# HGRN value unit moved behind the scores of the fourth NSA pair in the third block's mixer stage

## What is computed

```
h = x @ w_in
(q_n, kc, vc, ks, vs, kw, vw, g_n, q_m, k_m, v_m, conv_in, q_h, f_h, i_h, g_h) = jnp.split(h, split_points, axis=-1)
o_nsa  = nsa_attention(q_n, kc, vc, ks, vs, kw, vw, gates, rel_tab[:NSA_HEADS])
o_conv = conformer_conv(conv_in, dw_w, dw_b, cln_g, cln_b, pw_w)
o_hgrn = hgrn2_mixer(q_h, f_h, i_h, g_h, lb, hn_g)      # i_h: the values
mixed  = jnp.concatenate([o_nsa, o_moba, o_conv, o_hgrn], axis=-1) @ w_out
```

## Time and profile before

| what | value |
|---|---|
| median of 3 runs | 3122.36 us (3117.55 to 3126.65) |
| the profiled execution | 3120.94 us, its span 3119.1 us |
| TensorE matmul busy | 2967.4 us (95%) |
| DVE, ACT, POOL busy | 55%, 46%, 5% |
| mean granted TensorE clock | 0.97 of full |
| instructions | 53947 |

### The profile page before, as it was taken

One profiled execution on the slowest core, in us unless ns is written; L12 is line 12 of the kernel. 1 busy time (PEld: TensorE's weight loads), 2 busy tenths in 40 slices (PEclk: granted clock), 3 DMA queues, 4 the chain that ended last, 5 costly groups with the idle time before them and its releaser, 6 DMA issues.

```text
span 3119.1 us, 53947 instructions
## 1 busy us (share of the span) xinstructions
PE 2967.4 (95%) x23720; PEld 2757.1 (88%) x23720; DVE 1717.3 (55%) x2029; ACT 1434.4 (46%) x1831; POOL 164.1 (5%) x197
## 2 busy tenths in 40 slices
PE   8999998999999998999999999999889999999998
PEld 8988898999989898998989899898879899886887
DVE  5455555455454555455456654546685555474555
ACT  4455654445455654444445444444441344344444
POOL 1000100000000100001000000000010000054000
PEclk9999999999999999999999999999989999898999
DMA  6553334554543344555554455454320255340443
GB/s 244 186 187 127 131 137 162 189 189 176 189 176 136 122 145 165 187 182 215 189 200 166 151 186 188 177 189 150 136 82 4 84 180 187 142 164 32 156 178 135
DMA packets 69394, 492.89 MB, mean 158 GB/s; under 512 B 7853, under 2 KB 9421, under 8 KB 10534
## 3 DMA queue, kind: packets, MB, share of 16 engines
q1 hardware_dynamic: 64224, 465.53, 41.5%
q10 hardware_dynamic: 4938, 23.92, 2.0%
HBM read 488.32 MB, written 1.06 MB: 157 GB/s over the span
## 4 chain that ended last, share of the span: by engine, by line
PE 82%; DVE 8%; ACT 6%; POOL 2%; issue 2%; PEld 1%; DMA 0%; PEldq 0%; ACTq 0%; DVEq 0%; POOLq 0%; SPq 0%
PE bank L105 52%; PE acc L105 29%; ACT weights_hi L118 2%; DVE weights_lo L313 2%; POOL conv_gate L3102 1%; POOL conv_out L3105 1%; DVE tmp L673 1%; DVE h L666 1%; DVE h L681 1%; PEld acc L105 0%; DVE b_x_lo L733 0%; DVE b_x_lo L505 0%; PE acc L1005 0%; DMA weight_ring<-in_weights 0%; DVE tmp L613 0%
## 5 line engine op out<-in xcount | busy, mean ns | idle before, releaser
L313 DVE TENSOR_TENSOR weights_lo<-weight_ring,weights_hi 128x2048 fp32r<-128x2048 f32 x440 | 1009.7, 2295 | 946.1 <-ACT weights_hi L118 945.7
L105 PE MATMUL bank<-b_x_hi,weights_hi 128*128 128x256 f32 x3576 | 1017.7, 285 | 22.0 <-DVE b_x_lo L733 17.2
L105 PE MATMUL bank<-b_x_hi,weights_lo 128*128 128x256 f32 x3576 | 1012.3, 283 | 0.0
L105 PE MATMUL bank<-b_x_lo,weights_hi 128*128 128x256 f32 x3576 | 1011.6, 283 | 0.0
L118 ACT ACTIVATE weights_hi<-weight_ring 128x2048 fp32r<-128x2048 f32 x440 | 839.5, 1908 | 371.0 <-PE acc L105 355.8
L105 PEld LDWEIGHTS bank<-b_x_hi,weights_hi 128*128 128x128 f32 x3576 | 680.3, 190 | 35.0 <-issue 19.4
L105 PEld LDWEIGHTS bank<-b_x_lo,weights_hi 128*128 128x128 f32 x3576 | 680.4, 190 | 3.3
L105 PEld LDWEIGHTS bank<-b_x_hi,weights_lo 128*128 128x128 f32 x3576 | 679.4, 190 | 0.0
L105 PE MATMUL acc<-weights_hi,b_hidden_hi 128*128 128x512 f32 x832 | 329.9, 397 | 0.0
L105 PE MATMUL acc<-weights_hi,b_hidden_lo 128*128 128x512 f32 x832 | 328.5, 395 | 0.0
L105 PE MATMUL acc<-weights_lo,b_hidden_hi 128*128 128x512 f32 x832 | 327.6, 394 | 0.0
(11 more groups left out here) (487 smaller groups left out, 4019.0 us busy)
## 6 DMA issues: line engine op xcount, KB each, us to landing
weight_ring<-in_weights SPq DMA_DIRECT2D x440, 1024.0 KB, 4.8
xn<-in_norm_rows ACTq DMA_DIRECT2D x14, 1024.0 KB, 4.7
sgu_bias_row<-in_sgu_rows ACTq DMA_DIRECT2D x1, 2048.0 KB, 10.4
sgu_norm_rows<-in_sgu_rows ACTq DMA_DIRECT2D x1, 2048.0 KB, 9.7
bias_hankel<-bias_scratch ACTq DMA_DIRECT2D x1, 1536.0 KB, 6.5
h<-in_x SPq DMA_DIRECT2D x2, 512.0 KB, 6.6
mem_norm<-in_memory SPq DMA_DIRECT2D x1, 1024.0 KB, 13.8
sgu_w_spatial<-in_sgu_w_spatial ACTq DMA_DIRECT2D x1, 1024.0 KB, 4.7
```

What stands on the lines that cost most here:

```text
L105: return pe.matmul(out, a, b, start=start, stop=stop, skip_group_check=True)
L313: dve.tensor_tensor(k.w.lo[:, n % 2, :], k.ring[:, n % RING, :], k.w.hi[:, n % 2, :], ALU.subtract) \
```

## The change

One step of each of three lists moves later; nothing is added or removed. On TensorE the unit moves from behind `pe_turn` of ("nsa", 0) to behind `pe_nsa_scores(k, pe, 3)`. On ACT the copy of half 1 moves from behind `act_turn` of ("nsa", 0) to behind `act_scores` of ("nsa", 3). On DVE the copy of half 0 moves from behind the `lo` that follows `dve_turn` of ("nsa", 0) to behind `dve_compressed(k, dve, 1)`. The order of the units among themselves, and with it the loads, `hi` and `lo`, stays.

```diff
 pe_mixers
     pe_turn(k, pe, k.att3, ("nsa", 0), 0, True)
-    ap = unit(k, pe, *w3(I_H))
-    pe_at(k, pe, HI, ap, pe_tile_tok, 0, 0, ("took_dve", HI, 0))
-    pe_at(k, pe, HI, ap, pe_tile_tok, 1, 1, ("took_act", HI, 1))
-    unit_done(k, "tile", HI, 1)
     pe_compressed_turn(k, pe, 0)
...
     pe_nsa_values(k, pe, ("nsa", 0), 0, 0)
     pe_nsa_scores(k, pe, 3)
+    ap = unit(k, pe, *w3(I_H))
+    pe_at(k, pe, HI, ap, pe_tile_tok, 0, 0, ("took_dve", HI, 0))
+    pe_at(k, pe, HI, ap, pe_tile_tok, 1, 1, ("took_act", HI, 1))
+    unit_done(k, "tile", HI, 1)
     pe_nsa_values(k, pe, ("nsa", 1), 0, 1)
 act_mixers
     act_turn(k, act, att, ("nsa", 0), 0, True)
-    act_take(k, act, HI, 1, k.h_vt[:, 1, :], bank=k.bank[1][:, 0:S])
     act_compressed_turn(k, act, 0)
...
     act_scores(k, act, att, ("nsa", 3), 1, True)
+    act_take(k, act, HI, 1, k.h_vt[:, 1, :], bank=k.bank[1][:, 0:S])
     act_take_pair(k, act, ("nsa", 1), 0)
 dve_mixers
     lo(k, dve)
-    dve.wait_ge(*k.s.at("tile", HI, 0))
-    dve.tensor_copy(k.h_vt[:, 0, :], k.bank[0][:, 0:S]).then_inc(*k.s.up("took_dve", HI, 0))
     dve_taps(k, dve, 24, TAPS - 1)
...
     dve_max(k, dve, ("nsa", 3), 1)
     dve_compressed(k, dve, 1)
+    dve.wait_ge(*k.s.at("tile", HI, 0))
+    dve.tensor_copy(k.h_vt[:, 0, :], k.bank[0][:, 0:S]).then_inc(*k.s.up("took_dve", HI, 0))
     dve_nsa_weights(k, dve, 3)
```

## The result

The changed kernel takes 3129.76 us (median of 6 runs, 3126.91 to 3133.07) against 3120.57 us for the kernel before (6 runs, 3117.55 to 3127.03): ratio 1.0028, 95% interval 1.0016 to 1.0041. The forecast was 3126.2 us and "within 0.3%", so the measured time lies in the range and just inside the class, 3.6 us above the number. Taken together the change costs about 10 us, where the sum had 4.6. Every step of the mechanism can be found in the profile; its balance was wrong, and the rest of this document is about why.

The account below looks back on a forecast made before the run. POOL's convolution taps were taken to bound the kernel up to 2836.9 us, then TensorE. Terms 0.3 + 2.1 + 0 + 7.1 - 5.4 + 0.5 = +4.6 us gave 3125.5, with half the median's offset 3126.2 us; range 3118 to 3135.

Parts of the forecast that it names:

- The first part: Up to 2836.9 us, on POOL's taps: the removed 7.1 us become TensorE idle time, POOL is delayed 0.3 us.
- Rival C: POOL's taps slowed in full by DVE: 2.5 us instead of 0.3, +6.8 us in all, 3128 us; chance 0.1.
- Step (1): Second half of the convolution's sum and first value products: at the lower clock level from their start, +2.1 us.
- Step (2): Scores of ("nsa", 3): 7.50 us at the lower clock level, unchanged, 0.
- Step (3): The unit at its new place on TensorE: costs what it took at the old one, +7.1 us.
- Step (4): Value products through second gathered sums, behind the unit: clock up again, -5.4 us.
- Step (5): Second gathered sums: a new wait for DVE to empty bank 0, +0.5 us.
- Rival A: Unit and the 14 us behind it: clock does not come back, +12.7 us, 3134 us; chance 0.16.
- Rival B: Clock high throughout, value products and scores included: -2.6 us, 3118 to 3120 us; chance 0.14.

Follow-up runs that it names:

- e1: The changed kernel run again with no edit: 3128.58 us against 3116.28 us for the kernel before, ratio 1.0039.
- e5: The kernel before run again with no edit, for a second profile: 3120.5 us.
- e12: The kernel before run again with no edit, for a third profile: 3120.4 us.
- e10: The changed kernel with DVE's copy of the unit's first half ahead of the compressed maxima: a profiled length of 57.35 us against 57.50 in e1.
- e8: The kernel before with the unit cut from 48 to 6 matmuls at its old place: 3127.88 us against 3116.88 us.
- e9: The unit put just ahead of the convolution's sum, its copies moved along: 3120.05 us, ratio 1.0007 to the kernel before.
- e11: The kernel before with POOL's last six taps on DVE and the HGRN query unit's first half ahead of the compressed rows' turn: 3112.13 against 3117.23 us.
- e2: The changed kernel with POOL's last four convolution taps given to DVE: 3118.57 us.
- e3: The kernel before with POOL's last four convolution taps given to DVE: 3117.50 us.
- e7: The changed kernel with the unit cut from 48 to 6 matmuls at its new place: 3125.66 us, ratio 1.0031 to the kernel before.

## Why the prediction was right, and where it was not

**The first part** was right: POOL's taps held the place, most of the removed 7.1 us became idle time, and the waits came out at 4.9 and 3.2 us (2.3 and 2.7 in e1, where TensorE arrived later). POOL's own delay was 0.74 us, not 0.3. Its last two taps ran beside DVE's level products and weights, with products of 1.24 us (beside the level products) and 1.03 us (beside the weights) against 0.93 and 0.92 before. The Trainium skill ("GPSIMD Engine Reference", section 1, Specifications) has the two engines contend where VectorE reads two SBUF inputs; the trace agrees in direction for the level products, which read two such inputs, and 0.74 us is under a third of the 2.5 that a full stop for each of the six products would cost. Rival C was not it, though its 3128 us lies nearer the measured time than my number does.

**Step (1)**, the first value products at the lower level: +2.1 forecast, +2.2 measured against the first profile, +2.65 against e5 (in e1 +0.8 and +1.3).

**Step (2)** is the one that failed. It took the 7.50 us of the scores as what they cost in the kernel before, "unchanged: 0". That was true of the one profile that I had. In e5 and e12 they take 4.18 us, since there TensorE doesn't wait. The term is +3.3 us.

**Step (3)**: 7.1 us forecast; 6.5 in the first profile of the changed kernel and 14.54 - 7.5 = 7.0 in e1.

**Step (4)** failed for the same reason. "Given back" was the difference between 7.05 and 3.94 us, and 7.05 was again the wrong base: e5 has 4.03, the changed kernel 4.04, so nothing is given back. The gathered sums took 5.41 us, not 3.6, with the clock at 0.69; e5 has 5.15. In e1 they took 3.81, as forecast, so this part differs from one execution to the next. Without the turn, which is counted in step (5) here, -4.7 us were forecast; -2.8 appeared against the first profile and +0.3 against e5.

**Step (5)**: the turn and the wait through the copy are 0.83 us; against 0.70 in e5 that is +0.1, not +0.5. e10 agrees: taking the copy off the chain gained nothing that can be told from none.

Against e5 A's terms are: later start of the step behind the wait 0.6, then 2.65 + 3.3 + 6.5 + 0 + 0.1 + 0.3, together 13.5 us, and A differs by 61.7 - 48.2 = 13.5. Against the first profile it is 6.3, the size of my sum plus the gathered sums' 1.8. The means of the profiles (49.8 of three, 59.6 of two) differ by 9.8 us, about what the runs say: 9.2 and 12.3.

**Rival A** (the clock doesn't come back behind the unit) was not what happened: it did come back. **Rival B's** state, all at the upper level, exists, but in the kernel before, which makes the change dearer, not cheaper. I had counted a different clock only as an uncertainty of the changed kernel, never of the base. The forecast class "within 0.3%" holds by the first comparison by a hair, and the second has its centre outside. That the time fell into the range is partly luck: the sum gave +4.6 us where 9.2 and 12.3 were measured, and the range reached up to 3135 us on account of rival A, which did not occur.

On the clock itself, the trace shows 20.5 us of unbroken busy time at the lower level, ended by gathered sums. The Trainium skill ("TensorE: Matmul & The Clock Gate", Part 1, What's actually happening) says that the throttled state is the default and that activity releases it. The trace agrees that idle time goes with the fall, by the profiles with and without the wait. But it also shows that a busy record is not enough for the rise: value products, scores and compressed scores kept the engine busy for these 20.50 us at 0.50, while in e5 the same steps ran at 1.00 for 12 us from the convolution's sum on, where the clock was up already. What about these products makes the difference wasn't tried. Nor is it shown that the wait alone decides: the clock also changes at different points of the same work from one execution to the next. The unit at its old place, for one, took 7.1, 8.5 and 7.2 us in the three profiles of the kernel before, behind 1.4 to 1.6 us of idle time each.

## What to carry to other kernels

Before pricing a move, ask which engine sets the end of the stage that the work leaves: work taken from beside another engine's chain is worth nothing while that chain sets the end, and the idle time that it leaves can cost more than the work did, as e8 shows with 42 matmuls less and 11 us more, 1 us of them for another reason. Where two engines reach a meeting point within a microsecond of each other, one profile shows one side only, so take two or three of the base before its terms go into a sum. To fill such a wait use work that must be done anyway and put it ahead of the meeting point (e9, e11), or shorten the chain that is waited for (e2).

## What the runs showed of the hardware that I had not expected

- A wait of 0.88 us and the light products around it go with a fall to the lower level about 2.7 us after the wait, which then lasts 20.5 us. Without that wait the same products run at the upper level (e5, e12, e3, e9). The stretch from the first value products to the second gathered sums' end takes 25.2 us in the first profile and 17.7 in e5.
- Two executions of one program differ by 3.2 us in a piece of the kernel that is the same in both: the steps from 2699.5 to 2782.7 us of the first profile of before took 83.2 us there and 86.5 in most others. The total hides it: e5's stage is 7.8 us shorter than the first profile's, and its time, 3120.5 us, is 0.4 us less.
- Behind the small level products TensorE stands idle for 1.7 to 2.6 us at a time with no wait shown, in every kernel of this study. The sum of these gaps is largest where the unit is cut (4.0 us in e7 and 3.2 in e8, 2.1 to 2.7 in the others). What causes them is open.
